# Layer 1 recurrence: grams in four quarter tiles, last doubling level in 32x32 tiles, per-head group norm on VectorE

## The reference

```python
    def step(state, inp):
        r_t, d_t, k_t, v_t, kk_t, a_t = inp
        sa = jnp.einsum('bhvk,bhk->bhv', state, kk_t)
        state = (state * d_t[:, :, None, :] - sa[..., None] * (kk_t * a_t)[:, :, None, :]
                 + v_t[..., None] * k_t[:, :, None, :])
        return state, jnp.einsum('bhvk,bhk->bhv', state, r_t)
    ...
    ym = jnp.mean(y, axis=-1, keepdims=True)
    yv = jnp.mean(jnp.square(y - ym), axis=-1, keepdims=True)
    y = ((y - ym) * lax.rsqrt(yv + GN_EPS)).reshape(b, s, d) * lnx_g + lnx_b
    bonus = jnp.sum(rh * kh * r_k, axis=-1, keepdims=True) * vh
    y = (y + bonus.reshape(b, s, d)).astype(x.dtype)
    return (y * g) @ w_o
```

## Time and profile before

| what | us |
|---|---|
| median of 3 runs | 1399.68 (1394.99 to 1402.66) |
| the profiled execution | 1396.21 |
| its span, first to last instruction | 1394.4 |
| PE busy | 1352.9 (97%) |
| DVE busy | 434.1 (31%) |
| ACT busy | 277.7 (20%) |
| POOL busy | 93.9 (7%) |
| the recurrence, first gram to first projection | 743.8 to 851.9 |

### The profile page before, as it was taken

The page is one execution under the profiler, slowest core; times in us unless marked ns, Lnnn a source line. Parts: engine busy times, 40 slices in busy tenths (PEclk is TensorE's granted clock), DMA queues, the critical chain, the costliest instruction groups (busy, mean ns, idle before and its releaser), DMA issues.

```text
span 1394.4 us, 24696 instructions
## 1 busy us (share of the span) xinstructions
PE 1352.9 (97%) x10364; PEld 788.8 (57%) x10364; DVE 434.1 (31%) x932; ACT 277.7 (20%) x549; POOL 93.9 (7%) x124
## 2 busy tenths in 40 slices
PE   7999999999999999979999997999999999999997
PEld 6889443443444444349699997954344443434433
DVE  2245122221222222146643225622222232222213
ACT  1231211111111111113412333121111111111111
POOL 7202000000000000012004100300000000000001
PEclk9999999999999999999999999999999999999999
DMA  4697799999999999966232006579999999999993
GB/s 151 177 357 308 307 358 416 422 422 421 422 422 422 422 422 422 421 212 201 92 122 94 4 4 243 235 278 377 397 421 422 422 422 423 422 422 421 423 421 156
DMA packets 98666, 450.45 MB, mean 323 GB/s; under 512 B 16032, under 2 KB 45344, under 8 KB 48928
## 3 DMA queue, kind: packets, MB, share of 16 engines
q1 hardware_dynamic: 98592, 449.34, 80.4%
HBM read 448.26 MB, written 1.05 MB: 322 GB/s over the span
## 4 chain that ended last, share of the span: by engine, by line
PE 93%; DVE 4%; ACT 1%; issue 1%; DMA 1%; PEld 0%; SPq 0%; PEldq 0%; DVEq 0%; ACTq 0%
PE PS L1860 31%; PE PS L1899 16%; PE PS L1907 10%; PE PS L1831 7%; PE PS L549 4%; PE PS L512 3%; PE PS L1384 2%; PE PS L1361 2%; PE PS L1500 2%; PE PS L1346 2%; PE PS L1879 1%; PE PS L1519 1%; PE PS L1980 1%; PE PS L1515 1%; PE PS L1871 1%; PE PS L534 1%
## 5 line engine op out<-in xcount | busy, mean ns | idle before, releaser
L2212 DVE TENSOR_TENSOR y_parts<-PS,y_parts 128x512 fp32r<-128x512 f32 x128 | 88.5, 691 | 216.5 <-ACT y_parts L2114 216.5
L2186 DVE SCALAR_TENSOR_TENSOR AR<-AR,PS 128x256 f32<-128x256 f32 x64 | 30.8, 481 | 386.4 <-ACT AR L2092 386.4
L1907 PE MATMUL PS<-y_parts,token_map 128*128 128x512 f32 x496 | 146.6, 417 | 0.0
L1860 PE MATMUL PS<-AR,xT 128*64 128x512 f32 x512 | 115.7, 593 | 5.5 <-issue 5.5
L1907 PEld LDWEIGHTS PS<-y_parts,token_map 128*128 128x128 f32 x496 | 83.5, 188 | 60.9 <-issue 50.3
L1899 PE MATMUL PS<-AR 128*64 128x512 f32 x512 | 116.9, 598 | 0.0
L1899 PE MATMUL PS<-RING,AR 128*64 128x512 f32 x496 | 116.9, 598 | 0.0
L1860 PE MATMUL PS<-AR 128*64 128x512 f32 x512 | 115.5, 592 | 0.0
L2114 ACT CAST y_parts<-PS 128x512 fp32r<-128x512 f32 x128 | 75.0, 586 | 172.0 <-PE PS L1899 172.0
L1860 PE MATMUL PS<-RING,xT 128*64 128x512 f32 x480 | 108.1, 592 | 0.0
L1860 PE MATMUL PS<-RING,AR 128*64 128x512 f32 x480 | 108.1, 592 | 0.0
(11 more groups left out here) (315 smaller groups left out, 1602.8 us busy)
## 6 DMA issues: line engine op xcount, KB each, us to landing
RING<-in_moe_w_gate SPq DMA_DIRECT2D x64, 1024.0 KB, 11.8
RING<-in_moe_w_up SPq DMA_DIRECT2D x64, 1024.0 KB, 13.9
AR<-in_moe_w_gate SPq DMA_DIRECT2D x64, 1024.0 KB, 13.1
AR<-in_moe_w_up SPq DMA_DIRECT2D x64, 1024.0 KB, 15.2
AR<-in_moe_w_down SPq DMA_DIRECT2D x64, 1024.0 KB, 13.9
RING<-in_moe_w_down SPq DMA_DIRECT2D x62, 1024.0 KB, 15.0
AR<-in_ab_w_in SPq DMA_DIRECT2D x8, 1024.0 KB, 5.6
AR<-in_rw_w_o SPq DMA_DIRECT2D x4, 1024.0 KB, 5.5
```

Of the source, the lines that this page charges most:

```text
L1860: ins = nc.tensor.matmul(PS[s * B:(s + 1) * B, 4, :], gathered(k)[:, c:c + B], gate_and_up(slots[s])[:, k, :, :], start=(k == 0), stop=(k ...
L1907: ins = nc.tensor.matmul(PS[:, 2 * t + h, :], OHT[:, half, t, :], YS[:, n, h * 512:(h + 1) * 512], start=False, stop=True, skip_group_chec ...
L2186: nc.vector.scalar_tensor_tensor(out=HH[0:2 * B, :].rearrange("p (k j) -> p k j", k=FT), in0=by_row(SIL[0:2 * B, :]), scalar=GC[:, buf:buf ...
L2212: nc.vector.tensor_tensor(YS[:, 1, h * 512:(h + 1) * 512], PS[:, 5 + h, :], YS[:, 0, h * 512:(h + 1) * 512], ALU.subtract).then_inc(q["low ...
```

## The change

The grams of chunks 0 and 1, and those of 2 and 3, are computed together: `grams(pair, n)` issues for each `k` the two heads of the even and of the odd chunk, four calls on four quarters of the array, into two banks. There are 8 groups of 16 calls in place of 16 groups of 8. Their places on PE change: before the first product stand only the first kind (n = 0, 1) of chunks 0 to 3; the second kind follows between level blocks. The order of the masks on DVE and the waits are fitted to that.

At level 5 `product` and the turned inverse compute only the 32x32 block that is new, with tiles of 32 rows and 32 columns, and `factor` and ACT's copy take 32 columns of each head's 64.

The group norm's scaling runs on DVE alone: per head one instruction (x - mean) * weight and one * scale + residual, 32 for each t. Aggregates and variance are a function of their own, `moments`; for t = 0 it goes before `state(2)`, and `deviation(0)` on ACT goes before `y_out(2)`. ACT's `scale` is gone.

```diff
@@ -846,6 +845,23 @@
+        lower = [slice(0, 32), slice(CH, CH + 32)]
+        upper = [slice(32, CH), slice(CH + 32, P)]
+        first_part = [(0, 0), (0, 1), (1, 0), (1, 1)]
+        masked_order = first_part + [(2, 0), (3, 0), (2, 1), (3, 1), (0, 2), (1, 2), (0, 3), (1, 3), (2, 2), (3, 2), (2, 3), (3, 3)]
+        gram_order = [(0, 0), (0, 1), (1, 0), (1, 1), (0, 2), (0, 3), (1, 2), (1, 3)]
+        def masked_by(*grams):
+            return max(masked_order.index(g) for g in grams) + 1
+        def gram_bank(c, n):
+            if n < 2:
+                return (0, 4, 2, 6)[c] + n
+            return (2, 6)[c % 2] + n % 2
@@ -1010,11 +1026,12 @@
-            def masked(c, m, part, b):
-                v.wait_ge(r["gram_done"], 4 * c + 2 * m + part + 1)
+            def masked(c, n):
+                m, part = n // 2, n % 2
+                v.wait_ge(r["gram_done"], gram_order.index((c // 2, n)) + 1)
                 dst = (GMB, GMK)[m][c][:, 4 * part:4 * part + 4, :, :].rearrange("p k m t -> p k (m t)")
-                V.tensor_tensor(dst, PS[:, b, :].rearrange("p (k f) -> p k f", k=4), mask,
+                V.tensor_tensor(dst, PS[:, gram_bank(c, n), :].rearrange("p (k f) -> p k f", k=4), mask,
                                 ALU.mult).then_inc(r["gram_masked"], 1)
@@ -1022,7 +1039,9 @@
                 dst = XI[w] if lv else DG[w]
-                V.tensor_tensor(dst, bank(4 * w), SM[:, lv:lv + 1, :].to_broadcast([P, KT, CH]),
+                cols = slice(0, 32 if lv == LEVELS else CH)
+                V.tensor_tensor(dst[:, :, cols], bank(4 * w)[:, :, cols],
+                                SM[:, lv:lv + 1, cols].to_broadcast([P, KT, cols.stop]),
                                 ALU.mult).then_inc(r[f"factor_ready{w}"], 1)
@@ -1044,32 +1063,28 @@
-            def normed(t):
+            def moments(t):
                 link.sync()
...
+            def normed(t):
                 v.wait_ge(r["deviation_ready"], t + 1)
...
                 link.sync()
-                V.scalar_tensor_tensor(out=NB[:, t, :], in0=MVS[:, t, 8:16, 0], scalar=-1.0, in1=RS[:, t, 8:16],
-                                       op0=ALU.mult, op1=ALU.mult).then_inc(r["scales_ready"], 1)
+                v.wait_ge(r["residual_ready"], t + 1)
                 for part in range(2):
-                    y = YTK[:, t, 512 * part:512 * part + 512]
-                    if part == 0:
-                        yh = y.rearrange("p (h d) -> p h d", h=8)
-                        link(V.tensor_tensor(yh, yh, wide(MVS[:, t, 0:8, 0], 8), ALU.subtract))
-                        link.sync()
-                        link(V.tensor_tensor(yh, yh, wide(RS[:, t, 0:8], 8), ALU.mult))
-                        link.sync()
-                    else:
-                        v.wait_ge(r["scaled"], t + 1)
-                    link(V.tensor_tensor(y, y, LG[:, 512 * part:512 * part + 512], ALU.mult))
+                    heads = [(h, slice(h * HD, (h + 1) * HD)) for h in range(8 * part, 8 * part + 8)]
+                    for h, cols in heads:
+                        link(V.scalar_tensor_tensor(out=YTK[:, t, cols], in0=YTK[:, t, cols], scalar=MVS[:, t, h, 0:1],
+                                                    in1=LG[:, cols], op0=ALU.subtract, op1=ALU.mult))
                     link.sync()
-                    v.wait_ge(r["residual_ready"], t + 1)
-                    V.tensor_tensor(y, y, RES[:, t, 512 * part:512 * part + 512],
-                                    ALU.add).then_inc(r["normed_ready"], 1)
+                    for h, cols in heads:
+                        ins = V.scalar_tensor_tensor(out=YTK[:, t, cols], in0=YTK[:, t, cols], scalar=RS[:, t, h:h + 1],
+                                                     in1=RES[:, t, cols], op0=ALU.mult, op1=ALU.add)
+                    ins.then_inc(r["normed_ready"], 1)
@@ -1078,25 +1093,28 @@
-            for c in range(2):
-                for n in range(4):
-                    masked(c, n // 2, n % 2, 4 * c + n)
+            for g in first_part:
+                masked(*g)
             factor(0, 0)
+            masked(2, 0)
             factor(1, 0)
-            masked(2, 0, 0, 2)
-            masked(2, 0, 1, 3)
+            masked(3, 0)
             factor(0, 1)
+            masked(2, 1)
             factor(1, 1)
-            masked(2, 1, 0, 6)
-            masked(2, 1, 1, 7)
+            masked(3, 1)
+            masked(0, 2)
+            masked(1, 2)
             factor(0, 2)
+            masked(0, 3)
             factor(1, 2)
-            masked(3, 0, 0, 2)
-            masked(3, 0, 1, 3)
+            masked(1, 3)
+            masked(2, 2)
+            masked(3, 2)
             factor(0, 3)
+            masked(2, 3)
             factor(1, 3)
-            masked(3, 1, 0, 6)
-            masked(3, 1, 1, 7)
+            masked(3, 3)
             for lv in range(4, LEVELS + 1):
@@ -1119,10 +1137,12 @@
             solution(2)
+            moments(0)
             state(2)
...
             stats(1)
+            moments(1)
             normed(1)
@@ -1212,7 +1232,8 @@
                 s.wait_ge(r[f"turned_inverse_done{w}"], LEVELS * wave + lv)
-                A.copy(DT[c], bank(4 * w + 1)).then_inc(r[f"turned_inverse_ready{w}"], 1)
+                cols = slice(32 if lv == LEVELS else 0, CH)
+                A.copy(DT[c][:, :, cols], bank(4 * w + 1)[:, :, cols]).then_inc(r[f"turned_inverse_ready{w}"], 1)
@@ -1229,13 +1250,6 @@
-            def scale(t):
-                s.wait_ge(r["scales_ready"], t + 1)
-                for h in range(8):
-                    y = YTK[:, t, (8 + h) * HD:(9 + h) * HD]
-                    ins = A.activation(y, y, ACT.Identity, scale=RS[:, t, 8 + h:9 + h], bias=NB[:, t, h:h + 1])
-                ins.then_inc(r["scaled"], 1)
@@ -1263,15 +1277,13 @@
             inverse(3, 5)
+            deviation(0)
             y_out(2)
...
             A.activation(UU[:, NCH - 1, :, :], bank(3), ACT.Copy, scale=-1.0).then_inc(r["solution_ready"], 1)
-            deviation(0)
             y_out(3)
-            scale(0)
             deviation(1)
-            scale(1)
@@ -1317,7 +1329,7 @@
-            g.wait_ge(r["gram_masked"], 4 * c + 2)
+            g.wait_ge(r["gram_masked"], masked_by((c, 0), (c, 1)))
             low = GMB[c][:, :, 0, :]
@@ -1475,15 +1487,19 @@
-            def grams(c, m, part, b):
-                n = 4 * c + 2 * m + part
-                if n >= 8:
-                    pe.wait_ge(r["gram_masked"], {8: 3, 9: 4, 10: 7, 11: 8}.get(n, n - 3))
-                for k, h in core[8 * part:8 * part + 8]:
-                    cols = token_cols(h, c)
-                    ins = mm(PS[token_rows(h, c), b, (k % 4) * P:(k % 4) * P + P], (AT, KTT)[m][half_rows[h], k, cols],
-                             SGRT[half_rows[h], :, k, cols], start=True, stop=True)
+            def grams(pair, n):
+                if n >= 2:
+                    pe.wait_ge(r["gram_masked"], masked_by(*{(0, 2): ((2, 0), (3, 0)), (0, 3): ((2, 1), (3, 1)),
+                                                             (1, 2): ((0, 2), (1, 2)), (1, 3): ((0, 3), (1, 3))}[pair, n]))
+                m, part = n // 2, n % 2
+                for k in range(4 * part, 4 * part + 4):
+                    for c in (2 * pair, 2 * pair + 1):
+                        for h in range(2):
+                            cols = token_cols(h, c)
+                            ins = mm(PS[token_rows(h, c), gram_bank(c, n), (k % 4) * P:(k % 4) * P + P],
+                                     (AT, KTT)[m][half_rows[h], k, cols], SGRT[half_rows[h], :, k, cols],
+                                     start=True, stop=True)
                 ins.then_inc(r["gram_done"], 1)
@@ -1497,8 +1513,13 @@
                     rows = token_rows(h, c)
-                    ins = mm(PS[rows, 4 * w, col(k)], GMB[c][rows, k, 0, :],
-                             DG[w][rows, k, :] if lv else ident[rows, rows], start=True, stop=True)
+                    if lv == LEVELS:
+                        lo, hi = lower[(c % 2) ^ h], upper[(c % 2) ^ h]
+                        ins = mm(PS[hi, 4 * w, k * CH:k * CH + 32], GMB[c][lo, k, 0, 32:CH], DG[w][lo, k, 0:32],
+                                 start=True, stop=True)
+                    else:
+                        ins = mm(PS[rows, 4 * w, col(k)], GMB[c][rows, k, 0, :],
+                                 DG[w][rows, k, :] if lv else ident[rows, rows], start=True, stop=True)
                 ins.then_inc(r[f"product_done{w}"], 1)
@@ -1516,13 +1537,18 @@
                     rows = token_rows(h, c)
-                    ins = mm(PS[rows, 4 * w + 1, col(k)], XI[w][rows, k, :], DT[c][rows, k, :], start=True, stop=True)
+                    if lv == LEVELS:
+                        lo, hi = lower[(c % 2) ^ h], upper[(c % 2) ^ h]
+                        ins = mm(PS[lo, 4 * w + 1, k * CH + 32:(k + 1) * CH], XI[w][hi, k, 0:32], DT[c][hi, k, 32:CH],
+                                 start=True, stop=True)
```

(22 more changed lines are left out.)

3 lines of the change are left out of this document (1 added, 2 removed).

## The result

The changed kernel takes **1390.4 us** (median of 7 runs, 1387.4 to 1391.3) where the kernel before took 1402.3 beside it (7 runs, 1395.0 to 1405.6): ratio **0.9928, 95% interval 0.9912 to 0.9945**, a gain of about 10.1 us (7.7 to 12.3), worked out from the ratio. The ratio isn't the quotient of the two medians, which lie 11.9 us apart. The forecast was a gain of 10.7 us, that is a ratio of 0.9924. The profiled execution took 1387.4 us, its span is 1385.6.

The account below looks back on a forecast made before the run. TensorE's back-to-back matmuls were taken to bound the recurrence stage, and an earlier second projection to shift the following DMA stream. Gains 1.3 + 1.5 + 1.2 + 4.9 + 1.8 = 10.7 us gave 1389.0 us, range 1384 to 1397.

Parts of the forecast that it names:

- A: Recurrence stage from first gram to first transposes, 32.2 us before: cheaper grams, partly lost to idle time, gain 1.3 us.
- B: First transposes to the second pair's first product, 12.0 us before: 32x32 tiles at the last level gain 1.5 us.
- C: Second pair's first product to the end of the last result, 55.6 us before: 32x32 tiles gain 1.2 us.
- tail: End of the last result to the first projection, 8.35 us before: the group norm's rearrangement gains 4.9 us.
- clock: First projection, 15.95 us before: with a shorter hole ahead of it the granted clock doesn't fall, gain 1.8 us.
- part 1: Second part of normed(0)'s columns on DVE at the tail: forecast ready 1.4 us late, part 0 in time.
- the 27.5: PE's forecast matmul time in A, in us: 20.5 for 22 blocks and 7.0 for the grams.
- Rival 1: Idle PE at the stage's front (747 to 752 us) lowers the clock: 3.5 us lost, gain 7.2 us; chance 0.14.
- Rival 2: Grams: no more than two tiles run at a time, grams cost 6.6 us more, total gain 4.3 us; chance 0.08.
- rival 4: Gram quads wait for weight loads in a shared row group, 330 ns each: 3.4 us slower than before; chance 0.04.
- Rival 3: Norm on DVE dearer (0.27 us or more an instruction) and 32x32 blocks at no gain: gain 5.4 us; chance 0.09.

Follow-up runs that it names:

- second trace: The changed kernel as it is, profiled again beside the last experiment's kernel on the same chip: 1389.6 us, ratio 0.9928 to the kernel before.
- grams alone: The kernel before with only the gram part (groups of two chunks, order of masks and grams): 1399.6 us, ratio 0.9999.
- left as it was: The changed kernel without the 32x32 tiles at the last level: 1392.2 us, ratio 0.9953 to the kernel before.
- norm alone: The kernel before with only the norm part (moments before the state step, root before y_out(2), scaling per head on VectorE): 1392.3 us, ratio 0.9940.
- last level alone: The kernel before with only the 32x32 tiles of the last level: 1399.4 us, ratio 0.9998.

## Why the prediction was right

| term | predicted gain | in the profiles | shown by |
|---|---|---|---|
| A, grams | 1.3 | 1.05 (1.75 in the second trace) | grams alone: 0.65 |
| B, last level | 1.5 | 1.77 | left as it was: 12.00 again |
| C, last level | 1.2 | 0.83, by luck (see below) | left as it was: 54.29 |
| tail, norm | 4.9 | 4.78 | norm alone: 4.88 |
| clock | 1.8 | 1.87 | norm alone: 1.87 |
| sum | 10.7 | 10.3 | time: 10.1 |

**The tail and the clock** carry the result, and their steps held one by one: moments and root hidden, ACT's y_out(2) with 4.25 us to spare, per-head instructions 0.208 us apart (I took 0.20, from the row of the same operation and not from bn_stats), part 1 ready 1.47 us after the end of the last result (forecast 1.4), first projection 3.59 us after the last result (3.45), 14.1 us long at full clock. Norm alone gives both terms, so the cause is shown and not only argued. One premise of the clock term was a wrong reading. "The only falls in this trace follow stretches with little or no matmul work" isn't so: the clock also falls from 722.6 to 726.0, behind 16 us in which PE was full, so that its mean is 0.83 in the second of these windows:

```profile
716.00:720.00 4.00, 4.00 (x66) 3.83 (x60) 0.00 (x0) 0.37 (x1) 0.00 (x0) 1.00 0.02 2
720.00:724.00 4.00, 4.00 (x38) 3.98 (x39) 0.00 (x0) 0.18 (x1) 0.00 (x0) 0.83 0.91 344
```

All 13 traces have that fall. At the norm the step held: the three traces with the long hole (before, grams alone, last level alone) fall there, and of the ten with the short one only two do.

**A** came out right by luck, by two errors that cancel. PE idles 1.88 us between 749 and 755, not 3.3: 0.42, 0.07 and 1.39 where I had 0.5, 0.45 and 1.7, and nothing before the next gram group or for restarts. But the matmuls took 1.7 us more than the 27.5: the first block behind a wait took 1.17 us where a block in a row takes 0.93, later gram groups up to 1.1 instead of 0.88, and 0.7 us of it are slow records and one small hole on the grid (records 4774, 4902 and 5284) that the second trace doesn't have. The quads themselves are as forecast: 109 ns for four records of 128 columns. Of the 4.7 us that the grams save, 3.6 are gone, as forecast (3.3), but the lost cover took only 1.9 of them. And the mask wait, taken away, came back as a wait for instructions.

**B** gained more than forecast though the block was dearer (0.565 us, not 0.54): the pair before had cost 2.01 us, not 1.87, which I had used for the blocks and had then charged to the tile change.

**C is where a step failed.** "Four blocks in B and four in C save 1.55 us each": in C the blocks are shorter by 1.2 us, and C isn't. The rate of 17 ns a record is real, but PE can't be fed at that rate for long, and the two holes, 1.05 us, appear within it and right behind it. My sign for it, blocks near 0.54 us, held, and the gain was still not there; it should have been the mark, not the block. That C is 0.8 us shorter all the same is luck: without the 32x32 tiles it is 1.4 us shorter than before, and nearly all of that lies at four places of the grid. Before, four small holes of the same kind stand at records 6430, 6558, 6685 and 6813, with 0.47 us of idle time. A hole costs more than the idle time in the timeline, which counts from the modelled end of the matmul before it: from start to start PE took 0.28, 0.28, 0.34 and 0.44 us at these records, against 0.05 us in the kernel without the tiles. The four blocks of 32 records that hold them took 1.3 us more in all than there. Whether a part of the change keeps these holes shut or the execution does, no run shows; grams alone and norm alone, each with one of the four open and some idle time elsewhere, have a C 0.3 us shorter than before.

**The rivals.** Rival 1 (starved front with a clock fall): the changed kernel's clock stays at 1.00 in the stage in both traces. In the run with the masks moved it fell twice, at 3.4 us in all, close to the price named (3.5), though at level 5 of the second pair and at the norm and not at the front. In the run with 32 columns of both it fell once, at the norm's hole (first projection 15.69). So a fall can still come where none is forecast, and what decides it stays open. Rival 2 (four tiles bring nothing) and rival 4 (a quad of 330 ns) are refuted by the same row: 109 ns. (Rival 4 was the rule of the Trainium skill, TensorE: Matmul & The Clock Gate, Part 3, The mechanism; for these quads the trace disagrees. The same section excepts loads that go to the background weight buffer; no run here tells whether these do.) Rival 3 was half right: the norm was not dearer, but the 32x32 blocks of C came at no gain in C.

**The rest of the span** is unchanged (466.87 and 466.68), only shifted, as the wait of the DMA queue had said.

## What to carry to other kernels

When an engine looks busy and back to back, ask also at what rate its instructions can reach it: here some 27 to 31 ns for a matmul with its weight load, over a hundred of them or more, so smaller tiles pay only beside slower work (B) and not in a stretch that already runs at that rate (C). Count the records between waits that nothing explains; a constant distance that doesn't care what the instructions do is the sign, and a packet on the instruction queue that lands a constant time before PE goes on is the proof. And cost the end of a serial tail first: it was two thirds of this gain, and two parts that look like more matmul work saved were, alone, within the scatter.

## What the runs showed of the hardware

- **PE's instruction supply.** In 13 traces, every wait of PE over 0.1 us in A, B or C that has no releaser lies on one grid of 127.4 matmul records (moved as a whole by 32 records where code was put ahead). Between two such waits on neighbouring places of the grid lie 3.4 to 4.0 us, 27 to 31.5 ns a record; over four in a row it was 29.9. The DMA queue in the stretch of the two holes of the changed kernel:

```profile
DMA packets 3, 0.05 MB, mean 4 GB/s; under 512 B 0, under 2 KB 0, under 8 KB 0
q8 instruction: 3, 0.05, 2.2%
```

  Three packets in 824 to 835 us, one for each 127 records. (The Trainium skill, Advanced Engine Details and Errata, ISA Cache, gives a line of 16 KB with 256 instructions. The grid agrees: 127.4 matmuls with as many weight loads are 255 instructions. The section also says that there are only two lines, but gives 128 KB for TensorE. No run here counts the lines; the packets above come one piece ahead, as with two.)
- **Whether a hole opens varies between executions**: at record 7195 the changed kernel waited 0.39 us in one and 0.12 in another, and at 10356 0.15 and 3.13.
- **A clock fall needs no idle stretch before it**: in all 13 traces the granted clock falls to its lower level some 21 us ahead of the first gram (722.6 to 726.0 in the trace of before), behind windows in which PE was busy for 4.00 of 4 us. The same 0.66 us hole at record 7195 had a fall after it in one trace and none in another.
- **Tiles beside each other.** Four 64x64 tiles with 128 columns start within 20 ns of each other, the next four 109 ns later. Two 32x32 tiles start 6 to 7 ns apart, the next two 31 to 32 ns after the first. (The Trainium skill, TensorE: Matmul & The Clock Gate, Wait — 56ns, not 53.3ns?, says that start-to-start never drops below about 25 ns. For single starts the trace disagrees; the mean of a pair, 16 ns, is below it too.)
- **Weight columns set the time of a small block**: 32 records with 64 weight columns took 0.93 us with 64 or with 32 moving columns, and 0.51 with 32 of both. No run has 32 weight columns with 64 moving ones.
